# A hybrid retention and gated linear attention encoder layer with routed experts: branch products set between query and key projections ahead of the state products, and gates fetched by the weights' queue

## What is computed

```python
def _mixer(h, positions, w_in, ...):
    proj = h @ w_in
    rq, rk, rv, rg, gq, gk, gv, gr, ga, gate_logits = jnp.split(proj, split_at, axis=-1)
    ...
    ret = retention forward + retention backward over chunks of 128 tokens
    ret = (normed(ret) * ret_norm * silu(rg))
    ...
    gla = the same with decays log_sigmoid(ga @ gla_gate_w + b) / 16 per token and key column
    gla = (normed(gla) * gla_norm * silu(gr))
    g_ret, g_gla = jnp.split(jax.nn.sigmoid(gate_logits), 2, axis=-1)
    merged = g_ret * (ret @ w_branch_ret) + g_gla * (gla @ w_branch_gla)
    return merged @ w_out
```

## Time and profile before

| | us |
|---|---|
| median of 3 runs | 2877.21 |
| lowest and highest | 2873.48, 2881.25 |
| the profiled execution | 2878.35 |
| its span, first to last instruction | 2876.4 |

### The profile page before, as it was taken

How to read it: one execution, slowest core, us unless ns; L and a number is a source line. 1 busy time by engine, 2 the same in 40 slices (tenths; PEclk the granted TensorE clock), 3 DMA queues, 4 the chain that set the end, 5 groups by cost and what they waited for, 6 DMA issues and landing times.

```text
span 2876.4 us, 37049 instructions
## 1 busy us (share of the span) xinstructions
PE 2713.3 (94%) x13386; PEld 2317.0 (81%) x13386; DVE 2037.8 (71%) x2114; ACT 1646.2 (57%) x1548; POOL 280.2 (10%) x341
## 2 busy tenths in 40 slices
PE   7999899889899998993999999999999999999997
PEld 6888788778778776882888888888888888888886
DVE  7766434426546644437888898888898898889887
ACT  6334232234343322232778777877877777777776
POOL 0111010121011023100000000000000000000010
PEclk8999999999999999995999999999999999999998
DMA  4434131453334267425999999999999999999997
GB/s 152 134 104 142 45 102 38 97 113 55 73 110 80 52 154 198 146 111 217 348 383 384 370 385 384 387 374 385 379 387 376 383 374 387 382 373 382 387 388 281
DMA packets 263686, 719.35 MB, mean 250 GB/s; under 512 B 20044, under 2 KB 77516, under 8 KB 263600
## 3 DMA queue, kind: packets, MB, share of 16 engines
q1 hardware_dynamic: 227968, 622.01, 57.9%
q0 software_dynamic: 35632, 96.17, 13.0%
HBM read 648.90 MB, written 69.21 MB: 250 GB/s over the span
## 4 chain that ended last, share of the span: by engine, by line
PE 52%; DVE 1%; DMA 0%; issue 0%; ACT 0%; DVEq 0%; POOL 0%; POOLq 0%
PE e_gate_ps L2623 17%; PE e_up_ps L2623 17%; PE e_y_ps L2601 17%; PE e_turn L2577 1%; PE e_turn L2561 0%; DVE e_top_at L2442 0%; DVE e_top L2441 0%; DMA e_xg<-h_mid,e_token_next 0%; DVE e_silu L2444 0%; DVE e_act L2444 0%; DVE e_raw L2483 0%; DMA out_dram<-e_raw 0%; DVE e_xg L2537 0%; DVEq L2142 0%; ACT e_squares L2370 0%
## 5 line engine op out<-in xcount | busy, mean ns | idle before, releaser
L2430 DVE TENSOR_TENSOR e_part<-e_raw,e_part 128x2048 fp32r<-128x2048 f32 (+2 forms) x576 | 1196.4, 2110 | 176.6 <-ACT e_part L2350 174.8
L2350 ACT ACTIVATE e_part<-e_raw 128x2048 fp32r<-128x2048 f32 (+2 forms) x576 | 1008.9, 1773 | 310.2 <-PE e_y_ps L2601 168.0
L2601 PE MATMUL e_y_ps<-e_part,e_actT 128*128 128x512 f32 x2112 | 497.9, 392 | 0.1
L2623 PE MATMUL e_gate_ps<-e_part,e_xgT 128*128 128x512 f32 (+1 forms) x2304 | 496.4, 373 | 0.6 <-DVE e_xgT L2435 0.6
L2623 PE MATMUL e_up_ps<-e_part,e_xgT 128*128 128x512 f32 (+1 forms) x2304 | 489.0, 371 | 0.0
L2623 PEld LDWEIGHTS e_gate_ps<-e_part,e_xgT 128*128 128x128 f32 x2304 | 422.7, 189 | 61.9 <-issue 1.0
L2623 PEld LDWEIGHTS e_up_ps<-e_part,e_xgT 128*128 128x128 f32 x2304 | 421.7, 188 | 59.8
L2601 PEld LDWEIGHTS e_y_ps<-e_part,e_actT 128*128 128x128 f32 x2112 | 392.7, 188 | 79.7 <-issue 0.5
L105 PE MATMUL m_proj<-m_hT,m_w_part 128*128 128x512 f32 (+1 forms) x1380 | 328.7, 397 | 3.9 <-ACT m_lit L777 2.3
L105 PEld LDWEIGHTS m_proj<-m_hT,m_w_part 128*128 128x128 f32 (+1 forms) x1380 | 260.5, 189 | 61.7 <-issue 3.5
L105 PE MATMUL m_proj<-m_oT,m_w_part 128*128 128x512 f32 x768 | 208.9, 424 | 46.0 <-ACT m_stage L765 45.1
(11 more groups left out here) (367 smaller groups left out, 2509.4 us busy)
## 6 DMA issues: line engine op xcount, KB each, us to landing
e_raw<-in_w_down_dram SPq DMA_DIRECT2D x160, 1024.0 KB, 7.1
e_raw<-in_w_gate_dram SPq DMA_DIRECT2D x128, 1024.0 KB, 7.6
e_raw<-in_w_up_dram SPq DMA_DIRECT2D x128, 1024.0 KB, 8.8
e_raw<-in_w_gate_dram SPq DMA_DIRECT2D x64, 768.0 KB, 9.2
e_raw<-in_w_up_dram SPq DMA_DIRECT2D x64, 768.0 KB, 6.3
m_w_raw<-in_w_in_dram SPq DMA_DIRECT2D x54, 512.0 KB, 5.1
ret_sum<-m_stage POOLq DMA_DIRECT2D x64, 256.0 KB, 5.2
gla_sum<-m_stage POOLq DMA_DIRECT2D x64, 256.0 KB, 5.4
```

What stands on the lines that cost most here:

```text
L2350: nc.scalar.activation(part[k % PARTS][0][:, 0:size(k)], raw[k % RAW][:, 0:size(k)], ACT.Copy).then_inc(w_high, 1)
L2430: nc.vector.tensor_tensor(part[k % PARTS][1][:, 0:size(k)], raw[k % RAW][:, 0:size(k)], part[k % PARTS][0][:, 0:size(k)], ALU.subtract).th ...
L2601: ins = nc.tensor.matmul(y_ps[:, half, :], actT[i % 2][xi][:, c, :], w[wi][:, j * D + 512 * half:j * D + 512 * half + 512], start=(i, c, x ...
L2623: ins = nc.tensor.matmul(dst[:, half, 0:half_wide], xgT[xi][:, kc, :], w[wi][:, j * wide + half * half_wide:j * wide + (half + 1) * half_w ...
```

## The change

`middle_of` no longer holds A units. E8 to E15 of the previous head and A0, A1 of the next are put in one row ahead of the states: E8 E9 A0 E10 E11 E12 A1 E13 E14 E15. In the last head G0 and G1 take the place of A0 and A1, and G2, G3 stand behind the outputs; G4 and G5 go between the last 16 E units. E4 moves ahead of the key transposes. Two of the six weight splits of a head, the ones of the next head's value weights, stood behind A0 and A1; ACT and DVE now do both between E15 and S0. Before the first head, DVE splits the second block of value weights ahead of the first rope and not behind it. All gates are fetched by SP, between the weight loads; for a head, SP waits until the head before has used its own (`fetch_gates`). The 16 retention gates get four buffers of their own (`r_lit`), in the place of the values, once the last outputs are done. The merge loops run the same operations; the splits and `light` calls in them begin at unit 6 and no longer at unit 2.

```diff
     def middle_of(hd):
 
         s = [("S", hd, i) for i in range(NT - 1)]
-        a = [("A", hd + 1, i) for i in range(2)]
         z = [("Z", hd + 1, i) for i in range(4)]
-        if hd == HD - 1:
+        if is_ret(hd + 1) or hd == HD - 1:
             return s
-        if is_ret(hd + 1):
-            return [*s[0:2], a[0], *s[2:5], a[1], *s[5:7]]
-        return [*s[0:2], a[0], *s[2:4], z[0], *s[4:6], a[1], z[1], s[6], *z[2:4]]
+        return [*s[0:2], z[0], s[2], z[1], *s[3:5], z[2], s[5], z[3], s[6]]
+
+    def fill_of(hd, i):
+
+        return ("A", hd + 1, i) if hd + 1 < HD else ("G", 0, i)
+
+    def before_states(hd):
+
+        e = [("E", hd - 1, u) for u in range(8, 16)]
+        a = [fill_of(hd, i) for i in range(2)]
+        if hd == 0:
+            return a
+        return [*e[0:2], a[0], *e[2:5], a[1], *e[5:8]]
...
+    TAIL = [("E", HD - 1, u) for u in range(16)]
+    TAIL = [*TAIL[0:4], ("G", 0, 4), *TAIL[4:8], ("G", 0, 5), *TAIL[8:16]]
...
+            def fetch_gates(hd):
+                if hd:
+                    sp.wait_ge(lit_used, 4 * hd)
+                else:
+                    for n in range(4):
+                        sp.wait_ge(lit_stored[n], 16 * PAIRS)
+                for i in range(4):
+                    half = slice((i // 2) * HALF, (i // 2 + 1) * HALF)
+                    sp.dma_start(lit_sb[:, i], lit_dram[hd, i % 2, :, half]).then_inc(lit_in, 16)
+
+            def fetch_ret_gate(u):
+                if u >= 4:
+
+                    sp.wait_ge(r_used, 2 * (u // 2) - 2)
+                else:
+                    sp.wait_ge(out_done, NT * HD)
...
             for n in range(5, len(blocks)):
                 load(n)
+                if n == 6:
+                    fetch_gates(0)
+                kind, hd, i = blocks[n]
+                if kind == "E" and hd + 1 < HD and i:
+                    fetch_gates(hd + 1)
+                if blocks[n] in (("G", 0, 2), ("G", 0, 3)):
+                    for u in range(8):
+                        fetch_ret_gate(8 * (i - 2) + u)
...
             for hd in range(1, HD):
-                for u in range(8):
-                    add_sum(hd - 1, u)
-                for i in range(4):
-                    load_lit(nth_lit["C", hd, i])
-                for u in range(8, 16):
+                for u in range(16):
                     add_sum(hd - 1, u)
...
             for i in range(16):
-                if i >= EARLY_G:
+                if i >= 6:
                     light(i)
                 if i:
                     high_of_merged(i - 1)
-                if i >= EARLY_G and i % 2:
+                if i >= 6 and i % 2:
                     split_high()
...
+            split_low()
             for w in range(2):
                 rope_first(w)
-            split_low()
...
                 take_scores(hd, 0)
+                split_low()
                 take_scores(hd, 1)
+                split_low()
+                if is_ret(nxt):
+                    rope(nxt, 0)
+                    rope(nxt, 1)
                 split_low()
                 split_low()
```

More of the change, by code:

```diff
@@ L181, in mixer @@
         latest[s] = n
-    lit = [("C", hd, i) for hd in range(HD) for i in range(4)] + [("R", 0, u) for u in range(16)]
+    lit = [("C", hd, i) for hd in range(HD) for i in range(4)]
     FETCHED = len(lit)
@@ L990, in _ @@
                             exp_far(hd, 1, of_keys)
[L991 to L993 removed]
+                    take_sum(hd - 1, 4)
+                    if not gla:
                         take_keys(hd)
+                    take_sum(hd - 1, 5)
                     take_v(hd, 3)
@@ L997, in _ @@
                     split_high()
-                    for u in range(6 if gla else 4, 8):
-                        take_sum(hd - 1, u)
+                    take_sum(hd - 1, 6)
+                    take_sum(hd - 1, 7)
                     split_high()
-                    for u in range(8, 16):
-                        take_sum(hd - 1, u)
                 else:
@@ L1022, in _ @@
                 nc.scalar.activation(small[:, 1, :], small[:, 0, :], ACT.Sqrt).then_inc(rooted, 1)
[L1023 to L1028, removed]
+                if nxt < HD:
+                    for i in range(2, 4):
+                        take_qk(nxt, i)
+                    split_high()
                 for i in range(2):
@@ L1032, in _ @@
             for i in range(2, 4):
+                light(i)
+            split_high()
+            for i in range(2, 4):
                 high_of_flip(HD - 1, i)
-            for u in range(16):
-                take_sum(HD - 1, u)
-                if u % 8 == 7:
+            for u in TAIL:
+                if u[0] == "G":
+                    light(u[2])
+                else:
+                    take_sum(HD - 1, u[2])
+                if u in (("E", HD - 1, 7), ("E", HD - 1, 15)):
                     split_high()
+            split_high()
             def high_of_merged(i):
@@ L1994, in _ @@
                         score(hd, 3)
-                    for i in range(8, 16):
-                        branch(hd - 1, i)
                 else:
@@ L2003, in _ @@
                     score(hd, 1)
+                for u in before_states(hd):
+                    if u[0] == "E":
+                        branch(hd - 1, u[2])
+                    elif u[0] == "A":
+                        project_qk(nxt, u[2])
+                    else:
+                        project_lit(u)
                 for u in middle_of(hd):
@@ L2011, in _ @@
                 outputs(hd)
-                for i in range(2):
+                for i in range(2, 4):
                     if nxt < HD:
-                        project_qk(nxt, 2 + i)
+                        project_qk(nxt, i)
                     else:
@@ L2020, in _ @@
             flip(HD - 1, 3)
-            for i in range(16):
-                branch(HD - 1, i)
-            for i in range(EARLY_G, 16):
+            for u in TAIL:
+                if u[0] == "G":
+                    project_lit(u)
+                else:
+                    branch(HD - 1, u[2])
+            for i in range(6, 16):
                 project_lit(("G", 0, i))
```

100 lines of the change are left out of this document (35 added, 65 removed).

## The result

| | before | changed |
|---|---|---|
| median of 6 runs, us | 2876.36 | 2893.06 |
| lowest and highest | 2872.95, 2881.25 | 2889.96, 2897.83 |
| span of the profiled execution | 2876.4 | 2892.2 |

The changed kernel is slower: the ratio of the times is 1.0059, with a 95% interval from 1.0045 to 1.0072, that is 16.7 us between the medians (13 to 21 us by the interval) and 15.8 us between the profiled spans. The forecast was 2886.5 us, from a median of 2877.21 in three runs that is 2876.36 in six; the time lies inside the forecast's own range (2879 to 2894) and inside the wide one. Direction and mechanism were right. The size was too small: +9.3 us were forecast, 6.5 us less than between the profiled spans and 7.4 us less than between the medians.

What follows compares the result with a forecast made beforehand. PE's branch units were taken to be held up by four stage buffers, not arithmetic. Terms -39.0 + 3.2 + 32.0 - 8.6 + 19.2 + 2.5 = +9.3 us gave 2886.5 us on the median; own range 2879 to 2894, wide range 2865 to 2900.

Steps and rivals of the forecast that it cites:

- the wide one: Range over the forecast and its rivals, without rival 4 and the ends of rivals 2 and 3: 2865 to 2900 us.
- The step that decided: State stretches up to the outputs: value splits ahead of the first state add 32.0 us of wait, lower clock 19.2.
- Rival 2: At the new idle places the clock does not fall, or only for an instant: 2865 us, half of it 2872; chance 0.25.
- Rival 3: In heads 3 to 6 PE stays at 1.2 GHz from the first decay logit into the outputs: 2899 us; chance 0.18.
- Rival 4: Sums still hold up the branch units because their landing sets the pace; half of 39 us stays: 2906 us; chance 0.05.
- estimate of 2.6 us for a 256 KB transfer: Skill's rule for the sums: four stage buffers would never run out, and all of the 39.0 us would stay.
- The term of the E units: Branch stretches from behind the scores to the states: no unit waits for its stage buffer, -39.0 us; rope's bank hold, +3.2.
- PE's wait for the stage copies: Sign of being right: falls from 45.1 us to under 12, with the waits among value pieces staying.
- The rope's hold on the bank: Heads 1 and 2: DVE's rope must free a bank before a later branch unit starts; 0.8 us, four times, +3.2 us.
- The term of the end: End of the mixer: PE stands 8.9 us before a late gate logit, the clock falls; +2.5 us, give or take 3.
- The first head: First value products: DVE makes the second value block's low part first, so PE's 6.88 us wait goes; -8.6 us.
- SP's queue: Weight loads stand behind the gate fetch; a 6 us delay is hidden, beyond some 25 us costs fully; taken as nothing.

Runs made afterwards that it cites:

- E8: No run: a branch unit on PE, the first of the previous head's branch units in the row ahead of the states.
- E15: No run: a branch unit on PE, the last in the row ahead of the states; the change puts both value splits behind it.
- filler kernel: Changed kernel plus 6 useless products of 128x256 (14 in head 0) on PE behind the second state, into the output banks; 2872.65 us, ratio 0.9983.
- a_pool_gates: Changed kernel with the head gates fetched by POOL again, four in a row between two sums of branch units; 2900.43 us, ratio 1.0079.
- a_tail_late: Changed kernel with two gate units taken out from between the last branch units and put behind them; 2893.74 us, ratio 1.0045.
- a_lights_early: Changed kernel with ACT taking the later gate logits of the end three steps earlier among the high parts; 2893.56 us, ratio 1.0045.
- two filler runs: Changed kernel plus useless PE products behind the second state: 12 (24 in head 0), 2891.89 us; 6 (14 in head 0), 2872.65 us.
- a_splits_back: Changed kernel with DVE making both low parts of the next value weights behind a head's last state; 2852.45 us, ratio 0.9912.

## Why the prediction was right, and where it was short

**The step that decided was right.** The forecast said that the splits, put between E15 and S0, cost 32.0 us as a wait and 19.2 us as clock. Measured were 51.5 us together. The filler kernel takes them apart: 18.8 us of clock. The stretches without the clock are 111.24 us, with the 1.9 us that A0 waits in head 0 they are 113.1, and the forecast was 112.4. The changed kernel less the filler kernel gives 7.4 us of clock in heads 0, 1, 2 and 7 and 11.4 us in heads 3 to 6, forecast 7.2 and 12.0. Part of this closeness is luck: 1.8 and 3.0 us per head were picked out of 1.3 to 2.8 and 1.2 to 5.2 us, and what one head pays changes from one execution to the next. By heads: head 2 13.6 us (forecast 13.0), heads 3, 5 and 6 17.7 to 17.9 (18.2), head 4 19.2.

**Rival 2, no fall of the clock**, had 0.25. It is refuted by the clock of the windows (0.67 to 0.86 against 1.00 with filler) and by the 20 us. Its figure for half of the clock's cost, 2872 us, is an error of adding: the forecast's own terms give 2876. **Rival 3**, a clock that stays down from Z0 into the outputs, happened in one head of four in the profile, head 4, with 2.1 us more in its outputs; as a whole it did not hold. It was closer than that looks: in the profiled executions of three variants that leave the states as they are (`a_pool_gates`, `a_tail_late`, `a_lights_early`) three heads of the four ran so, with 2.4 us more in the outputs of each. Their eight state stretches sum to 128.1 to 130.4 us, as in the changed kernel. **Rival 4**, sums that hold up the E units all the same, is refuted: 59 units in 89.2 us. The estimate of 2.6 us for a 256 KB transfer, worked out from the Trainium skill, DMA: Bandwidth & Descriptors, section Anatomy of one DMA, is not borne out here: the profile after has a median of 4.8 us for the gla sums, before 5.4.

**The term of the E units was mis-sized by 2.9 us.** It said that no unit would wait for its stage buffer. In these stretches none does, but A0 waits, by way of ACT, for its own weights. ACT in head 2, the split of A0's block, and PE at A0:

```profile
515.92 1.06 ACT L704 ACTIVATE m_w_part<-m_w_raw 128x1024 fp32r<-128x1024 f32 x1 [2.12 <-DMA m_w_raw<-in_w_in_dram]
...
517.61 5.72 PE L105 MATMUL m_proj<-m_hT,m_w_part 128*128 128x512 f32 x24 [1.73 <-ACT m_stage L778]
```

In head 3 A0 starts 5.7 us behind the scores (616.37 to 610.72) and stood some 22 us behind them; its block, which SP may load only when the split two blocks earlier is done, lands only then. In head 2 ACT waits 2.12 us for it with E8's copy queued behind the split; PE waits 1.73 us, and 5.2 us in heads 1, 2, 3 and 5 together. That is part of why PE's wait for the stage copies did not fall under 12 us, as the forecast named for a sign of being right: of the 20.4 us, 10.6 lie among the value pieces as expected, 5.2 are these, and 4.6 belong to the E units of the last head. The forecast costed what the A units do for the E units, not what their own supply needs. A part of it came back since a unit of 24 products is 5.44 us in this row by the starts (626.02 to 631.46 in head 3), where I had taken 5.60. It is not the gate fetch ahead of the load: with the fetches back on POOL the same place waits 1.93 us. The rope's hold on the bank was 0.75 us once and 0.74 us three times, forecast 0.8 four times.

**The term of the end was short by 3.6 us.** PE there, rows of the changed kernel:

```profile
1105.42 4.58 PE L105 MATMUL m_proj<-m_oT,m_w_part 128*128 128x512 f32 x12 [2.20 <-ACT m_stage L778]
...
1136.85 4.48 PE L105 MATMUL m_proj<-m_oT,m_w_part 128*128 128x512 f32 x12 [2.35 <-ACT m_stage L778]
...
1162.36 46.16 PE L105 MATMUL m_proj<-m_hT,m_w_part 128*128 128x512 f32 x192 [10.16 <-ACT m_lit L790]
```

The wait ahead of G8 is 10.16 us (forecast 8.9). What was left out is the slow row behind the two shorter waits: the E units behind 2.20 and 2.35 us of idle take 4.58 and 4.48 us for 12 products where 12 take 2.80 at full clock, 3.5 us together. I had the price in the earlier trace rows and used it only for the long wait. The other deviations there, such as 10.16 us for 8.9, nearly cancel.

**The first head** gave 9.4 us in the profile, 8.2 alone by the medians, forecast 8.6. **SP's queue** costs nothing that the runs show: the kernel before with SP's fetches gains 24.6 us by the medians and 24.7 us in the E stretches alone.

## What to carry to other kernels

An instruction of 1.2 us that nobody needs soon must not stand ahead of a chain whose every link another engine waits for: two splits per head, moved behind the last state, were worth 40.6 us here, more than the 39.0 us of waits that the change was made to remove. Before an idle stretch is costed, look at what the granted clock does behind idle stretches of that length in the same trace, and add that to each of them, short ones too; it may go either way, so take a range. When two edits attack one wait, run each alone: here the spread row gave 32.0 and the fetches 24.7 of the 32.4 us that both give, and the fetches cost nothing elsewhere that the runs show.

## What the hardware did that I had not expected

Useless products made the kernel faster: 56 of them in the idle places, 2.75 us for six, held the granted clock at 1.00 in all eight heads and gave back 20.4 us (2893.06 to 2872.65, measured beside kernels before of 2876.36 and 2878.43). The Trainium skill says in TensorE: Matmul & The Clock Gate, Part 1, that only activity holds the gate open. The two filler runs, with 1.00 in all eight state stretches, agree.

The length of one idle stretch does not tell whether the clock falls. With one split moved it was 1.00 behind 1.83 us in five heads and fell behind 1.92 us in a sixth. Among the value pieces of heads 4 to 7, behind 2.64 or 2.65 us of idle, the six matmuls took 2.90 us in all four heads of the kernel before, but 1.61 to 1.63 us in three of the four in `a_splits_back`. And in head 7 the same row of states, behind the same idle, in the changed kernel and then in `a_pool_gates`:

```profile
1067.15 6.65 PE L1910 MATMUL m_work<-m_v,m_kw 128*128 128x256 f32 x20 [2.97 <-DVE m_states L1193]
```

```profile
1071.07 5.33 PE L1919 MATMUL m_work<-m_v,m_kw 128*128 128x256 f32 x20 [2.96 <-DVE m_states L1199]
```

The granted clock of the stretch is 0.86 in the first and 1.00 in the second; `a_tail_late` and `a_lights_early` have 1.00 there too. So a fall at every one of the new idle places, as the forecast took it, is what the changed kernel's profile shows and not a certainty. Where the clock did fall, a plain head paid 1.3 to 2.4 us, inside the forecast's 1.3 to 2.8.

Once it has fallen, a chain with many short waits can stay at 0.50 up to the outputs (head 4, 0.67 on the mean with S0 and S1 still at full clock), while heads 5 and 6, with the same instructions, came back within 9 us.
